# The opening of a three-block transformer kernel: order of its first loads, of GpSimd's first two lows and of one reciprocal

## What is computed

```python
def first_block(x, c, positions, w_ada, b_ada, ...):
    mod = jnp.einsum("bd,de->be", jax.nn.silu(c), w_ada[l]) + b_ada[l]
    shift1, scale1, gate1, shift2, scale2, gate2 = jnp.split(mod[:, None, :], N_MOD, axis=-1)

    h = layer_norm(x) * (1.0 + scale1) + shift1
    t = token_mixer(h, positions, w_in[l], b_in[l], ...)
    ...

def token_mixer(h, ...):
    proj = jnp.einsum("bsd,de->bse", h, w_in) + b_in
    q, k, v, g_ret, c_val, c_gate, gate_a, gate_b = jnp.split(proj, IN_SPLITS, axis=-1)
    a = c_val * jax.nn.sigmoid(c_gate)
    ...
```

## Time and profile before

| | |
|---|---|
| median of three runs | 3649.16 us (3644.05 to 3657.96) |
| span of the profiled execution (first to last instruction) | 3639.2 us |
| what lies around the span, against the median | about 10 us |
| TensorE busy, share of the span | 3330.8 us, 92% |
| tokens landed, means start | 24.48 us |
| modulation rows on VectorE | 35.6 to 58.3 us |
| first scaling step | 61.98 us |
| first dense matmul | 64.85 us |

### The profile page before, as it was taken

How to read it: one execution, slowest core, us unless ns; L and a number is a source line. 1 busy time by engine, 2 the same in 40 slices (tenths; PEclk the granted TensorE clock), 3 DMA queues, 4 the chain that set the end, 5 groups by cost and what they waited for, 6 DMA issues and landing times. The chain is left out here.

```text
span 3639.2 us, 42261 instructions
## 1 busy us (share of the span) xinstructions
PE 3330.8 (92%) x17094; PEld 2632.6 (72%) x17094; DVE 1662.8 (46%) x2602; ACT 1167.5 (32%) x1891; POOL 975.2 (27%) x418
## 2 busy tenths in 40 slices
PE   4999889989999799999999777989999888889998
PEld 2887767866888588888787664368887664568887
DVE  5895467554331323345500897532211585622211
ACT  2222364324443322122232224333223324533222
POOL 0000322432444122322232110024443220024443
PEclk8999999998999799999999998989999988989999
DMA  4232334451233122334321000012232110013332
GB/s 179 93 99 87 127 105 153 151 173 59 98 97 96 63 87 89 125 130 133 127 76 53 30 18 7 1 64 99 96 110 87 53 47 27 1 59 98 99 93 87
DMA packets 91198, 315.99 MB, mean 87 GB/s; under 512 B 10742, under 2 KB 12534, under 8 KB 90234
## 3 DMA queue, kind: packets, MB, share of 16 engines
q1 hardware_dynamic: 88060, 303.69, 25.8%
q10 hardware_dynamic: 2944, 9.60, 0.7%
HBM read 311.16 MB, written 2.10 MB: 86 GB/s over the span
## 5 line engine op out<-in xcount | busy, mean ns | idle before, releaser
L245 POOL TENSOR_TENSOR terms<-streams,terms 128x1024 fp32r<-128x1024 f32 (+2 forms) x414 | 975.0, 2355 | 2642.0 <-ACT terms L233 2642.0
L454 PE MATMUL bank<-terms,terms 128*128 128x512 f32 (+2 forms) x3936 | 1477.4, 375 | 44.7 <-DVE terms L721 18.2
L455 PE MATMUL bank<-terms,terms 128*128 128x512 f32 (+2 forms) x3936 | 1468.6, 373 | 0.0
L456 PE MATMUL bank<-terms,terms 128*128 128x512 f32 (+2 forms) x3936 | 1466.4, 373 | 0.0
L233 ACT ACTIVATE terms<-streams 128x1024 fp32r<-128x1024 f32 (+1 forms) x462 | 475.5, 1029 | 1792.3 <-PE bank L456 1605.3
L454 PEld LDWEIGHTS bank<-terms,terms 128*128 128x128 f32 x3936 | 748.8, 190 | 197.0 <-issue 45.0
L456 PEld LDWEIGHTS bank<-terms,terms 128*128 128x128 f32 x3936 | 749.1, 190 | 128.9
L455 PEld LDWEIGHTS bank<-terms,terms 128*128 128x128 f32 x3936 | 750.4, 191 | 123.3
L1642 DVE TENSOR_TENSOR stage<-stage,bank 128x256 f32<-128x256 f32 (+1 forms) x88 | 54.6, 621 | 596.4 <-ACT stage L1632 596.4
L1085 DVE SCALAR_TENSOR_TENSOR arena<-arena,vec 128x512 f32<-128x512 f32 x240 | 162.5, 746 | 0.2
L1625 DVE TENSOR_TENSOR terms<-stage,terms 128x512 fp32r<-128x512 f32 (+1 forms) x66 | 116.5, 1768 | 0.0
(11 more groups left out here) (333 smaller groups left out, 3120.2 us busy)
## 6 DMA issues: line engine op xcount, KB each, us to landing
streams<-in_ffn_w SPq DMA_DIRECT2D x104, 512.0 KB, 3.5
streams<-in_w_mod SPq DMA_DIRECT2D x72, 512.0 KB, 3.5
streams<-in_w_up SPq DMA_DIRECT2D x44, 512.0 KB, 3.5
streams<-in_w_gu SPq DMA_DIRECT2D x44, 512.0 KB, 3.5
streams<-in_w_ada SPq DMA_DIRECT2D x32, 512.0 KB, 3.5
streams<-in_w_down SPq DMA_DIRECT2D x32, 512.0 KB, 3.6
streams<-in_w_v SPq DMA_DIRECT2D x24, 512.0 KB, 3.8
streams<-in_ffn_w SPq DMA_DIRECT2D x24, 384.0 KB, 3.2
```

The costliest lines, as they stand in the source:

```text
L245: gp.tensor_tensor(self.low(m), self.raw(n), self.high(m), ALU.subtract).then_inc(self.low_made.sem, 1)
L454: pe.matmul(out, high[:, at], x_high, start=kk == start, stop=False)
L455: pe.matmul(out, high[:, at], x_low, start=False, stop=False)
L456: mm = pe.matmul(out, low[:, at], x_high, start=False, stop=kk == kts - 1)
```

## The change

Five edits, all in Start and FirstNorm:

- The tokens are loaded in two halves of four tiles each, SyncE issuing the first half ahead of all its other loads, ScalarE the second half in the place of the whole.
- The condition and the early rows stand behind them on SyncE's queue, otherwise in the order of before.
- x_loaded counts 32 instead of 16.
- GpSimd waits for all 16 early rows (mod_done) before its first low.
- The reciprocal stands ahead of row 12 on VectorE, and no longer behind the gain step.

```diff
     def __init__(self, k):
         self.k = k
-        self.counts = {k.loaded: 16 * 8, k.x_loaded: 16, k.c_loaded: 16, k.c_made: 1, k.constants: 9}
+        self.counts = {k.loaded: 16 * 8, k.x_loaded: 32, k.c_loaded: 16, k.c_made: 1, k.constants: 9}
...
+    def tokens(self, eng, half):
+        k, n = self.k, DT // 2
+        tiles = slice(n * half, n * half + n)
+        eng.dma_start(k.X[:, tiles, :], k.ap["x_t"].rearrange("(k p) t -> p k t", p=P)[:, tiles, :]
+                      ).then_inc(k.x_loaded.sem, 16)
+
     def sync(self, sp):
         k, ap = self.k, self.k.ap
+        self.tokens(sp, 0)
         sp.dma_start(k.arena[:, B1_C:B1_C + D], ap["c_rows"]).then_inc(k.c_loaded.sem, 16)
...
     def scalar(self, act):
         k = self.k
-        act.dma_start(k.X, k.ap["x_t"].rearrange("(k p) t -> p k t", p=P)).then_inc(k.x_loaded.sem, 16)
+        self.tokens(act, 1)
...
     def gpsimd(self, gp):
+        gp.wait_ge(self.k.mod_done.sem, EARLY)
         for m in range(PARTED):
             self.k.make_low(gp, m)
...
         for t in range(EARLY):
             if t % 4 == 0:
+                if t == EARLY - 4:
+                    self.inverse(dve)
                 dve.wait_ge(k.early_in[t // 4].sem, 16)
...
         dve.wait_ge(*k.gained(2))
-        self.inverse(dve)
         self.scaling(dve)
```

## The result

| | before | after |
|---|---|---|
| median, five runs each | 3649.16 us | 3631.88 us |
| lowest to highest | 3644.05 to 3657.96 | 3629.05 to 3638.03 |
| ratio, with its 95% interval | | 0.9948 [0.9936, 0.9961] |
| profiled execution: span | 3639.2 | 3636.2 |
| first scaling step | 61.98 | 47.73 |

The change is 0.5% faster; 3635.1 us was forecast. The median and the range of before are the same over its five runs as over the three named ahead of the prediction. The dense matmuls start 14.25 us earlier, where 14.1 was forecast. The two spans differ by only 3.0 us, though: the profiled execution of after (3638.03 us) was the longest of its five, and that of before (3640.97 us) was shorter than any of the five above. The last part of the experiments takes this up. The sure reading is therefore that of the opening, event by event.

What follows compares the result with a forecast made beforehand. The opening, a chain in which TensorE stands idle, was taken as the bound: rows' end -13.5, first scaling -0.8, second low +0.2, total -14.1 us, so 3635.1 us, range 3626 to 3645.

Steps and rivals of the forecast that it cites:

- The loads' order carries it, the tokens come at about 9.3: Opening loads: tokens first, in halves on both queues, land at 9.3 instead of 24.48; the rows' start gains 10.2 us.
- Even queues, the condition with group 1 at 15.5: Opening loads: condition's 4 KB packets alternate with group 1's 16 KB ones, both landing at 15.5; chance 0.45.
- Rows of 1.15 us pitch: VectorE's 16 modulation rows, freed of GpSimd's lows, take 18.4 us against 22.7: gain 4.3.
- Reciprocal 1.0 us with no wait: VectorE, ahead of the last four rows: root done at 36.8, 2.4 us to spare, so it costs only 1.0 us.
- The bias wins, the gain step waits: 2.9 us behind the rows: Behind the rows: only the gain step waits out the first low, first scaling 2.9 us behind the rows.
- The upper bound: Behind the rows: bias and gain both wait out lows, first scaling 5.0 us behind the rows.
- The sum: Whole opening: rows' end -13.5, first scaling -0.8, second low +0.2, total -14.1 us, giving 3635.1 us.
- SyncE ahead: Rival on the load queues: SyncE's half starts about 0.5 us or more earlier; 16.5 us gained, 3632.7 us; chance 0.3.
- lows winning twice: Rival behind the rows: first scaling 5.0 us behind them, 2 us back on any case; one in three of each.
- main case: The predicted case for the opening: even queues, 3635.1 us, chance 0.45.
- 10 us around the span: Whole time: the same 10 us lie around the profiled span in both kernels, 3625.1 of span giving 3635.1 us.
- The chance of more than 0.5%: Whole time: faster by 0.5% (18.2 us) 0.22, same 0.75, slower 0.03.

Runs made afterwards that it cites:

- loads alone: Only the new order of loads against before, GpSimd's lows and the reciprocal where they were: 3631.70 us, ratio 0.9956 [0.9942, 0.997].
- lows-alone kernel: Before with only GpSimd's wait for all 16 early rows added; one run, 3657.29 us, first dense matmul at 64.26.
- second interval: The changed kernel measured again, 8 runs, against before: 3636.56 us, ratio 0.9969 [0.9955, 0.9982].
- split kernel: After with five token tiles on SyncE's queue and three on ScalarE's instead of four each; one run, 3647.66 us.

## Why the prediction was right, and where it was right by luck

- **The loads' order carries it, the tokens come at about 9.3.** Right: 10.00, and loads alone give 13.8 us. The packet times of the earlier trace rows carried over.
- **Even queues, the condition with group 1 at 15.5.** Wrong, and this is the step that failed. SyncE's queue led by a microsecond; the condition came at 10.75 and group 0 at 20.6 instead of 25.3. The rival had the condition at 11, group 0 at 21 and the first row near 21.3. The sign was in the earlier trace rows and was named: the condition on that queue was through at 4.9 in before.
- **Rows of 1.15 us pitch.** Right: eight of them from 20.62, then a wait of 1.13 for group 2, which no case had. Forecast at 30.2, group 2 landed at 31.0; the rows reached it at 29.9 because they started so early.
- **Reciprocal 1.0 us with no wait.** Cost right (38.35 - 37.48 = 0.87), the wait was there. The rival had "root 36.8, reciprocal to 37.8, four rows to 42.4"; measured 37.45, 38.35 and 42.95, the half microsecond being piece 1's landing (high at 34.71).
- **The bias wins, the gain step waits: 2.9 us behind the rows.** Wrong: both wait, 47.73 - 42.95 = 4.8. The upper bound was given as 5.0, though its terms add up to 5.12. GpSimd starts 30 ns ahead of the bias step (43.03, 43.06), and 20 ns ahead in the lows-alone kernel (53.58, 53.60). The rule quoted from the Trainium skill (SBUF — State Buffer, "Who interferes with whom"), that the two exclude each other for the whole instruction, whoever issues first, held for every step with two SBUF inputs that met a low. The gain step has only one SBUF input, so the rule as quoted did not speak of it, and it waited all the same. The part was worth nothing: 4.3 us given, 4.3 taken. Of the up to 2.1 us that the sum was to lose, 1.9 came. The second low's 0.2 us among the low terms did not come, since both lows were over by then.
- **The sum.** That it came out at -14.1 against -14.25 is luck: the two wrong steps cancelled. The rows ended at 42.95, 1.85 earlier than forecast, and the small steps took 1.9 longer. The rival "SyncE ahead" with the lows winning twice would have given 16.5 - 2 = 14.5. The trace follows that rival within 0.7 us at every event it names, and not the main case; only the wait for group 2 was in neither.
- **10 us around the span.** Wrong. In all runs the time is 1.8 to 1.9 us above the span (3638.03 and 3636.2). The median of before lay 10 us above its profiled execution's span since that execution was a short one. Measured from median to median the assumption cancels, and the forecast came within 3.2 us.
- **The chance of more than 0.5%.** 0.22 was given; measured were 0.52% and then 0.31%, one on either side of the bound. The opening's 14.25 us are 0.39%. That lies inside the second interval and at the very edge of the first, so the first measurement may hold some luck of the clock as well.

## What to carry to other kernels

Order the opening's loads by packet size as well as by need: spread the urgent one evenly over both hardware queues, so that nothing with large packets stands beside it, and put the next small one right behind. Before GpSimd's work is moved, ask which steps of VectorE then stand beside it. Best is a place where VectorE waits anyway or runs steps that take no harm from a low (here the reciprocal and those that read a bank), or VectorE does the work itself (1.2 us a low against 2.3). A root, a table load or any step that needs nothing more goes ahead of the steps on its engine that wait for a transfer.

## What the runs showed of the hardware

- The two queues send nearly the same number of packets whatever their size: 47 to 43 between 16 KB and 2 KB packets, 66 to 66 between 4 KB and 2 KB.
- Of two loads issued within 10 ns of each other (0.73 and 0.74 us), that of SyncE moved its first packets before 2 us and that of ScalarE only after 3 us, in before, in after and in the split kernel. In the kernel with all tokens on SyncE it was the other way round: ScalarE's 16 KB packets moved before 2 us, the tokens' after 2.5. What decides it stayed open.
- In that same kernel the issues of the two early loads on SyncE took 4.72 and 4.85 us, where 0.4 to 0.5 is usual, and SyncE came to piece 0's issue at 11.52 instead of 2.82. In after it was two of the small tables whose issues took 7.84 and 9.76 us. Much lay in the queue each time; that this is the cause was not tested.
- A step of 8 columns by a constant (gain, one SBUF input) waited out a low like a two-input one (2.26 us against 0.17), while a reciprocal (0.94 us) and steps with a bank as second input (0.69 us each) ran at full pace beside a low.
- The exclusion works both ways: a low takes 2.34 us by itself, and 3.1 to 3.3 us among the rows of before, where it waits for the row that is running.
